# Weight ring of a two-layer hybrid kernel: one packed load and one split per stage, seven slots, steps written out

## The reference

```python
def swiglu(h, w1, w3, w2):
    return (jax.nn.silu(h @ w1) * (h @ w3)) @ w2

def moe_swiglu(h, w_router, w1, w3, w2):
    logits = (h @ w_router).astype(jnp.float32)
    top_v, top_i = lax.top_k(logits, TOP_K)
    gates = jax.nn.softmax(top_v, axis=-1)
    combine = jnp.sum(jax.nn.one_hot(top_i, N_EXPERTS) * gates[..., None], axis=-2)
    out = jnp.zeros_like(h)
    for e in range(N_EXPERTS):
        out = out + combine[..., e:e + 1] * swiglu(h, w1[e], w3[e], w2[e])
    return out
```

## Time and profile before

| | us |
|---|---|
| median of 3 runs | 1781.75 (1781.06 to 1784.72) |
| the profiled execution's own time | 1780.91 |
| its span | 1779.3 |
| PE busy in the span | 1611.2 |
| DVE busy | 1311.3 |
| ACT busy | 1051.8 |
| DMA queue of the weights (q1) | 425.28 MB, 60.9% of 16 engines' span |

### The profile page before, as it was taken

How to read it: one execution, slowest core, us unless ns; L and a number is a source line. 1 busy time by engine, 2 the same in 40 slices (tenths; PEclk the granted TensorE clock), 3 DMA queues, 4 the chain that set the end, 5 groups by cost and what they waited for, 6 DMA issues and landing times.

```text
span 1779.3 us, 26243 instructions
## 1 busy us (share of the span) xinstructions
PE 1611.2 (91%) x9274; PEld 1380.6 (78%) x9274; DVE 1311.3 (74%) x1194; ACT 1051.8 (59%) x1031; POOL 110.6 (6%) x146
## 2 busy tenths in 40 slices
PE   6888969999798897999998998998998998998994
PEld 6877859999787786787787787787787787787783
DVE  4888564444558856788788787887887887887885
ACT  4534454434362444577676676776776776776773
POOL 1152100000014210100000000000000000000000
PEclk9999989999899997899999999999999999999997
DMA  6429035533342002798898798897996996996993
GB/s 227 158 103 371 16 118 213 202 152 118 119 157 72 25 1 119 283 370 356 330 382 354 310 373 330 350 376 288 381 376 271 404 377 263 404 371 276 387 375 123
DMA packets 68113, 457.36 MB, mean 257 GB/s; under 512 B 7280, under 2 KB 8464, under 8 KB 16608
## 3 DMA queue, kind: packets, MB, share of 16 engines
q1 hardware_dynamic: 59696, 425.28, 60.9%
q0 software_dynamic: 8224, 31.36, 4.6%
q10 hardware_dynamic: 144, 0.05, 0.0%
HBM read 432.54 MB, written 24.12 MB: 257 GB/s over the span
## 4 chain that ended last, share of the span: by engine, by line
PE 66%; DVE 12%; DMA 9%; ACT 7%; issue 4%; SPq 1%; ACTq 0%; POOL 0%; DVEq 0%; POOLq 0%
PE bank L385 24%; PE bank L410 15%; DMA ring<-in_moe_w 8%; PE bank L388 7%; PE bank L1150 7%; PE bank L653 6%; PE bank L414 4%; ACT wh L454 3%; DVE wl L458 3%; PE bank L685 1%; PE bank L398 1%; DVE ml L640 1%; PE bank L1155 1%; DVE hs L1894 1%; DVE rw L1796 1%
## 5 line engine op out<-in xcount | busy, mean ns | idle before, releaser
L458 DVE TENSOR_TENSOR wl<-ring,wh 128x2048 fp32r<-128x2048 f32 x369 | 844.0, 2292 | 227.8 <-ACT wh L454 217.1
L454 ACT ACTIVATE wh<-ring 128x2048 fp32r<-128x2048 f32 x369 | 705.1, 1915 | 162.9 <-DMA ring<-in_moe_w 49.4
L385 PE MATMUL bank<-wh,xh 128*128 128x512 f32 x896 | 361.8, 404 | 12.6 <-DVE wl L458 11.1
L385 PE MATMUL bank<-wh,xl 128*128 128x512 f32 x896 | 351.3, 392 | 0.0
L385 PE MATMUL bank<-wl,xh 128*128 128x512 f32 x896 | 349.6, 390 | 0.0
L410 PE MATMUL bank<-wh,gh 128*128 128x512 f32 x448 | 183.0, 408 | 38.5 <-DVE gl L546 37.5
L385 PEld LDWEIGHTS bank<-wh,xh 128*128 128x128 f32 x896 | 168.4, 188 | 50.6 <-issue 19.5
L385 PEld LDWEIGHTS bank<-wh,xl 128*128 128x128 f32 x896 | 168.2, 188 | 37.3
L385 PEld LDWEIGHTS bank<-wl,xh 128*128 128x128 f32 x896 | 169.0, 189 | 32.1
L410 PE MATMUL bank<-wl,gh 128*128 128x512 f32 x448 | 180.3, 402 | 0.0
L410 PE MATMUL bank<-wh,gl 128*128 128x512 f32 x448 | 180.1, 402 | 0.0
(11 more groups left out here) (304 smaller groups left out, 2456.2 us busy)
## 6 DMA issues: line engine op xcount, KB each, us to landing
ring<-in_moe_w SPq DMA_DIRECT2D x336, 1024.0 KB, 7.3
ring<-in_ffn_w SPq DMA_DIRECT2D x33, 1024.0 KB, 5.2
ring<-in_w_in SPq DMA_DIRECT2D x24, 1024.0 KB, 4.9
ring<-in_w_out SPq DMA_DIRECT2D x8, 1024.0 KB, 4.7
job_x<-xrow POOLq DMA_DIRECT2D x1, 8192.0 KB, 27.7
job_y<-xrow POOLq DMA_DIRECT2D x1, 8192.0 KB, 46.3
job_y<-yj POOLq DMA_DIRECT2D x8, 512.0 KB, 8.6
xrow<-job_x POOLq DMA_DIRECT2D x7, 512.0 KB, 11.4
```

What stands on the lines that cost most here:

```text
L385: ins = nc.tensor.matmul(up_bank(run, par, 0)[:], x[:, 0:C], w[b][:, k], **kw)
L454: nc.scalar.activation(o, src[0], ACT.Copy).then_inc(sem("w_high"), 1)
L458: nc.vector.tensor_tensor(split(wl[:, buf]), src[0], split(wh[:, buf]).bitcast(F32), ALU.subtract).then_inc(sem("w_split"), 1)
```

## The change

Each stage's weights are packed by the host into one tile of 128 rows of 2048 numbers (`stage_tiles`): for an up stage the two halves of w1 and w3 side by side in the order in which the matmuls read them, for a down stage the rows of w2. A stage is one load of 1 MB into one slot, and one split with flat source and result. The stages are stored in the order in which they are split: up(0,0), up(0,1), up(1,0), up(1,1), down(0), up(2,0), up(2,1), down(1), and so on; in a job that follows another, its up(0,0) comes before the last down of the job before. The ring has seven slots, taken in the fixed order `ORDER`, and the load of stage i waits for the split of stage i - 7 alone. A job has 42 stages, six times round the ring. The inner loops over pairs on ScalarE, VectorE and SyncE are gone: the steps are written out in the loop over jobs. TensorE's program stays as it is. SyncE reads two expert numbers per job, since the loop now loads the old job's last down in its place. The room for the seventh slot comes from `fin`, the final norm's row, which now lies in `trig`.

```diff
-SLOTS = 6
-
-UP, DOWN = ((4, 5), (2, 3)), (1, 0)
+SLOTS = 7
+
+ORDER = (4, 5, 6, 1, 2, 3, 0)
+STAGE = 8 * T
...
-        fin = sb("fin", [P, D])
+        fin = trig[:].rearrange("p a t -> p (a t)")
...
-            def load(self, slot, half_m):
-                return 16 * (self.loads(slot) + half_m + 1)
+            def place(self, i):
+                slot = ORDER[i % SLOTS]
+                return slot, 16 * (self.loads(slot) + i // SLOTS + 1)
...
+        def split_high(act, run, i, buf, used=None):
+            stage = run.stages + i
             wait(act, "stage_used", stage - 2 if used is None else used)
+            slot, n = run.place(i)
+            act.wait_ge(sem(f"w_ready{slot}"), n)
+            nc.scalar.activation(wh[:, buf], flat_slot(slot), ACT.Copy).then_inc(sem("w_high"), 1)
+
+        def split_low(dve, run, i, buf, used=None):
+            dve.wait_ge(sem("w_high"), run.stages + i + 1)
+            nc.vector.tensor_tensor(wl[:, buf], flat_slot(run.place(i)[0]), wh[:, buf].bitcast(F32), ALU.subtract
                                     ).then_inc(sem("w_split"), 1)
...
         def act_steps(act, run):
             up, down = act_split(act, run)
 
-            def step(m, half_m, half_next, par):
+            for m in range(1, run.pairs - 1):
                 act_gated_high(act, run, m - 1)
-                up(m + 1, half_next, 1 - par, 0)
-                act_silu(act, run, m, par)
-                up(m + 1, half_next, 1 - par, 1)
-                down(m, half_m, par)
-
-            steps(act, run, step)
+                up(m + 1, 0)
+                act_silu(act, run, m, m % 2)
+                up(m + 1, 1)
+                down(m)
...
+            def stages(run, w, row, at, after_mixer=0):
+                for i in at:
+                    slot, _ = run.place(i)
+                    if after_mixer and i < SLOTS:
...
+                    else:
+                        sp.wait_ge(sem("w_split"), run.stages + i - SLOTS + 1)
+                    load(slot, flat_slot(slot), w[bass.ds(row + i * P, P), :])
...
             with sp.Fori(1, n_jobs) as j:
-                e = sp.value_load(jt[0:1, bass.ds(j, 1)], min_val=0, max_val=NE - 1)
-                sp_ffn(job(j), w1, w3, w2, e * (PAIRS_E * P), 0)
+                row, prev = expert(j), expert(j - 1)
+                run = job(j)
+                slot, _ = run.place(-1)
+                sp.wait_ge(sem("w_split"), run.stages - SLOTS)
+                load(slot, flat_slot(slot), A["moe_w"][bass.ds(row, P), :])
+                slot, _ = run.place(0)
+                sp.wait_ge(sem("w_split"), run.stages - SLOTS + 1)
+                load(slot, flat_slot(slot), A["moe_w"][bass.ds(prev + end * P, P), :])
+                stages(run, A["moe_w"], row, range(1, end))
+            j = last_job(sp)
+            stages(job(j), A["moe_w"], expert(j), (end,))
```

More of the change, by code:

```diff
@@ L354, in last_split @@
             def last_split(self, slot):
-                m = max(q for q in range(self.pairs) if q % 2 == parity(slot))
-                return 1 + (self.down(m, m == self.pairs - 1)[0] if slot in DOWN else self.up(m, 1)[0])
+                return 1 + max(i for i in range(3 * self.pairs) if ORDER[i % SLOTS] == slot)
         dense = Run(PAIRS_D, False, 0, 0, 0, lambda s: before(1, s))
@@ L459, in split_low @@
                                     ).then_inc(sem("w_split"), 1)
         def splitter(eng, fn, run):
[L462 to L473, removed]
+            def up(m, part):
+                early = run.follows and m == part == 0
+                i = -1 if early else part if m == 0 else 3 * m - 1 + part
+                fn(eng, run, i, run.up(m, part)[1], run.stages - 3 * run.pairs + 1 if early else None)
@@ L474, in splitter, with down @@
+            def down(m, last=False, followed=False):
+                i = 3 * run.pairs - 1 + followed if last else 3 * m + 4
+                fn(eng, run, i, run.down(m, last, followed)[1], run.used() - 3 if followed else None)
             return up, down
@@ L500, in act_start @@
             up, down = act_split(act, run)
[L501 removed]
+            up(1, 1)
             act_silu(act, run, 0, 0)
[L503 to L512, removed]
+            down(0)
         def act_steps(act, run):
             up, down = act_split(act, run)
[L517 removed]
+            for m in range(1, run.pairs - 1):
                 act_gated_high(act, run, m - 1)
[L519 to L524 removed]
+                up(m + 1, 0)
+                act_silu(act, run, m, m % 2)
+                up(m + 1, 1)
+                down(m)
         def act_end_a(act, run, followed=False):
@@ L549, in dve_start @@
             up, down = splitter(dve, split_low, run)
-            up(1, 0, 1, 1)
+            up(1, 1)
             dve_gate(dve, run, 0, 0)
-            down(0, 0, 0)
+            down(0)
         def dve_steps(dve, run):
             up, down = splitter(dve, split_low, run)
-            def step(m, half_m, half_next, par):
+            for m in range(1, run.pairs - 1):
                 dve_gated_low(dve, run, m - 1)
[L559 to L564, removed]
+                up(m + 1, 0)
+                dve_gate(dve, run, m, m % 2)
+                up(m + 1, 1)
+                down(m)
         def dve_end_a(dve, run, followed=False):
@@ L2102, in column_tiles, with stage_tiles @@
     return np.ascontiguousarray(np.swapaxes(w, -3, -2)).reshape(*w.shape[:-3], P, KT * n)
-def row_tiles(w):
-    w = np.asarray(w)
-    w = w.reshape(-1, 2, P, D)
-    return np.ascontiguousarray(np.swapaxes(w, 1, 2)).reshape(-1, 2 * D)
-def up_tiles(w):
-    w = np.asarray(w)
-    w = w.reshape(w.shape[-3], KT, P, w.shape[-1] // T, T)
-    return np.ascontiguousarray(w.transpose(0, 3, 2, 1, 4)).reshape(-1, KT * T)
+def stage_tiles(w1, w3, w2):
+    w1, w3, w2 = (np.asarray(w) for w in (w1, w3, w2))
+    e, pairs = w1.shape[0], w1.shape[-1] // T
+    up = np.stack([w1.reshape(e, 2, 4, P, pairs, T), w3.reshape(e, 2, 4, P, pairs, T)], 5)
+    up = up.transpose(0, 4, 1, 3, 2, 5, 6).reshape(e, pairs, 2, P, STAGE)
+    down = w2.reshape(e, pairs, 2, P, D).transpose(0, 1, 3, 2, 4).reshape(e, pairs, P, STAGE)
+    out = np.empty((e, 3 * pairs, P, STAGE), np.float32)
+    for m in range(pairs):
+        for part in range(2):
+            out[:, 3 * m - 1 + part if m else part] = up[:, m, part]
+        out[:, 3 * m + 4 if m < pairs - 1 else 3 * pairs - 1] = down[:, m]
+    return out.reshape(-1, STAGE)
 def weights(inputs):
```

94 lines of the change are left out of this document (30 added, 64 removed).

## The result

The changed kernel takes **1721.14 us** (median of 4 runs, 1720.83 to 1721.71) against 1781.4 for the kernel before (4 runs, 1778.29 to 1784.72). The ratio is 0.9662, 95% interval 0.9644 to 0.968. Forecast was 1722 us. The profiled execution has a span of 1719.2 us, 60.1 less than before.

A forecast was written before the change was run, and what follows sets the result against it. Expert jobs run near TensorE's pace, but each of seven job changes costs 11.2 us, 8.4 of it removable (idle, clock, shortage): 1780.9 - 58.8 = 1722 us, range 1712 to 1745.

The forecast's parts named there:

- The walk: Engine-by-engine trace of one change of job, around 970 us: idle 4.08, clock 2.06, shortage 2.5, together 8.6 us removable.
- The DMA wait at nothing: Weight loads at the job change: 15.5 us of lead covers even the slowest 12.0 us landing, so no wait remains.
- What is then last: TensorE before the down matmuls at a job change: idle falls from 5.58 to 1.50 us, early split still ahead of `gl`.
- The clock: TensorE's clock at the job change stays up after the shorter idle, so 2.06 us go from the next twelve matmuls.
- The second shortage: Late loads behind a job change, up to TensorE's restart at 1009.96: 2.20 us plus 0.3 for restarting, both to nothing.
- Splits and steps at nothing: Flat splits on ScalarE and VectorE, and loops written out: no difference in time; the steady pair stays at 8.43 us.
- B: At each job change the written-out loop's jump back stalls ScalarE and VectorE on a code fetch: 10 us, 1732, chance 0.27.
- C: The stretch behind a job change still starves by 2.5 us, so 17 us stay: 1739 us, chance 0.12.
- D: Memory gives no more than a job's mean 349 GB/s, so nothing is gained: 1781 us, chance 0.04.
- E: Code fetch at the jump back waits behind queued weight loads, up to 12.0 us: 27 us slower, 1808, chance 0.05.
- lower end: Bottom of the range: the last 1.50 us of TensorE idle per job change goes too, 10 us less, 1712.

## Why the prediction was right

**The place and the size.** It read 11.2 us lost per change of job and 8.4 of them as removable; 8.53 went. At the change of job that it walked, the parts measured are 4.25 us of idle (5.58 less 1.33), 1.89 us of clock (4.78 less 2.89) and 2.38 us of shortage, together 8.52. The walk had 4.08, 2.06 and 2.5, together 8.64. Of its own parts:

- *The DMA wait at nothing.* Right: 4.46 us of idle on ScalarE went, and the slowest load of the jobs took 8.2 us against the 15.5 us of lead.
- *What is then last.* The walk gave an idle of 1.50 us on TensorE, because of the early split ahead of `gl`; 1.33 was measured, with the rows of VectorE in the order foretold. VectorE does its three splits and reaches `gl` in 6.69 us (957.94 to 964.63), where 6.87 had been added up.
- *The clock.* Taken as kept, by the nearest row: kept at 1.33 us (window 1.00), lost again at 5.88 us when the wait was put back. The twelve matmuls were put at 2.72 us and took 2.89, since at the full clock too the first ones behind an idle come slower: the second starts 0.34 us behind the first (965.11 to 965.45), against 0.23 with no idle in front (961.43 to 961.66 in the run with VectorE's order turned round). This 0.17 us and the 0.17 by which the idle was put too long cancel; that is luck, worth 1.2 us over the seven changes.
- *The second shortage*, 2.5 us: gone. From the new job's first up matmul to the first of its fourth pair it took 24.51 us (985.45 to 1009.96, rows 9) and takes 22.42 (972.25 to 994.67); the twelve matmuls there took 3.01 us behind their wait and take 2.72: 2.09 and 0.29, together 2.38. The order alone left most of it; the packing and the written-out steps took it (2.24 us).
- *Splits and steps at nothing.* Right: VectorE's splits mean 2292 ns before and after, and the steady pair stayed at 8.43 us. The two pairs right behind a change of job take 8.40 and 8.41 us, the next ones 8.44 and 8.43 (rows below), and so on to the last turn before the next change, at 1194.03: nine pairs in 75.91 us, 8.43 each.

The chain of waits of the changed kernel, behind the change at 965 us and behind the one at 1086:

```profile
994.67 2.72 PE bank L383 x12
...
1101.31 0.22 PE bank L396 x2
...
1109.71 0.22 PE bank L396 x2
...
1118.12 0.22 PE bank L396 x2
...
1126.56 0.22 PE bank L396 x2
...
1134.99 0.22 PE bank L396 x2
```

**The rivals.** B, a fetch of code at the jump back, did not come about with loops of 167 and 146 instructions; it was seen on SyncE with a loop of 376, and in no loop of up to 311 instructions on ScalarE. Its price was put too low, if ScalarE's would be SyncE's: at the 4.1 to 5.9 us measured there, less the 1.9 us of work, an estimate of B is 7 x (2.2 to 4.0), 15 to 28 us, and not 10. No row of before could tell whether B would come, since its loops were of 68 and 52 rows; that it didn't was a bet that came out and was not worked out. C (the shortage stays) did not come about; the order alone, which leaves the shortage, gives 1736.49 where 1739 was worked out for C. D (transfers are the limit) is refuted by 373 GB/s held over whole jobs, where a job before had 349. E fell with B.

**What the prediction did not say** is how little of the change was needed: the order of the loads at a change of job, 45 us; the packing and the written-out steps together, 15; the seventh slot, nothing. Nor that the 1.5 us it left standing could be had by moving two instructions on VectorE; its lower end, 1712, has that idle gone without an edit that does it, and 1711.26 was measured with one.

## What to carry to other kernels

In a ring of loads, compare for each load the time from its issue to its first use with its time to landing, and do this at the joints (a change of job, of layer, of expert) and not in the steady stretch: a load that stands in the queue behind one that is needed later, or waits for a slot that is coupled to another, costs there what the steady stretch never shows. When the stall is taken away, walk the queues of the engines to the next wait before choosing an edit; moving `gl` alone gained at most 1 us, moving it and the gate together gained 10. An idle of TensorE of 5.6 to 5.9 us cost its clock on top, here 1.7 to 1.9 us each time (twelve matmuls in 4.55 to 4.78 us instead of 2.89).

## What the runs showed of the hardware that was not expected

- Code was brought in again at every round of a long loop on SyncE. Its loops of 376 and of 535 instructions made 32 and 39 packets of about 8 KB (0.26 MB / 32) in about six and a half rounds; loops of up to 311 instructions on ScalarE made none (one packet at most in the whole stretch). On SyncE the next instruction stands 0.3 us behind the jump back without such packets and 4.1 to 5.9 us behind it with them. Whether the limit is one of length between 311 and 376, differs by engine, or hangs on where the loop lies in the program, no run parted.
- The time from issue to landing is no fixed price of a load of 1 MB. It was 7.4 us at the median and 12.0 at most in the kernel before, at a mean of 349 GB/s over a job, and 5.0 and 8.2 in the changed kernel at 373. Asking for one megabyte at a time does not by itself give this: the run with SyncE's loop at 535 instructions does that too, at 370 GB/s, and its loads take 7.2 and 9.7 us. What sets it was not parted.
